# Attention loop of a two-layer block: value products one step later, two output units side by side, scores that wait tile by tile

## The reference

```
for i in range(1, N_BRANCH):
    acc = acc + jax.nn.sigmoid(proj(u, 'gate%d' % i)) * (ys[i] @ w_branch[i])
return acc @ w_out
```

## Time and profile before

| | |
|---|---|
| runs shown | 2553.7, 2552.97, 2550.1 us, median 2552.97 |
| the profiled execution | 2551.63 us, span 2549.8 us |
| mean granted TensorE clock | 0.988 |
| TensorE busy | 2430.2 us (95%) |
| VectorE busy | 1583.0 us (62%) |
| ScalarE busy | 1066.0 us (42%) |
| loop of A0 / B0 / C0 / D0 | 521 to 640 / 683 to 788 / 835 to 938 / 975 to 1052 us |
| loop of A1 / B1 / C1 / D1 | 1958 to 2043 / 2073 to 2131 / 2169 to 2224 / 2247 to 2294 us |

### The profile page before, as it was taken

The page is one execution under the profiler, slowest core; times in us unless marked ns, Lnnn a source line. Parts: engine busy times, 40 slices in busy tenths (PEclk is TensorE's granted clock), DMA queues, the critical chain, the costliest instruction groups (busy, mean ns, idle before and its releaser), DMA issues.

```text
span 2549.8 us, 31764 instructions
## 1 busy us (share of the span) xinstructions
PE 2430.2 (95%) x12584; PEld 1972.5 (77%) x12584; DVE 1583.0 (62%) x2620; ACT 1066.0 (42%) x1842; POOL 27.3 (1%) x43
## 2 busy tenths in 40 slices
PE   6999998999999999989999989999989999988998
PEld 3888886877767676668888868888868788768998
DVE  2799878345355447678898784333365466578654
ACT  5222234355444444462222342222354555556344
POOL 0000000000000000000000000000000000000000
PEclk9999999999999999999999999999999999998999
DMA  5555554221221112124555523222233243233554
GB/s 232 189 208 206 187 187 144 100 74 67 96 70 67 58 66 91 60 98 174 214 210 183 192 101 107 99 98 87 95 117 136 80 145 117 87 117 124 182 176 155
DMA packets 98069, 331.42 MB, mean 130 GB/s; under 512 B 11009, under 2 KB 12033, under 8 KB 97281
## 3 DMA queue, kind: packets, MB, share of 16 engines
q1 hardware_dynamic: 97922, 329.39, 36.7%
HBM read 323.06 MB, written 6.29 MB: 129 GB/s over the span
## 4 chain that ended last, share of the span: by engine, by line
PE 88%; DVE 5%; ACT 4%; issue 2%; DMA 1%; SPq 0%; POOL 0%; DVEq 0%; ACTq 0%
PE ps L347 26%; PE ps L338 24%; PE ps L339 23%; PE ps L649 5%; PE ps L1180 3%; PE ps L1155 3%; PE ps L1165 3%; ACT w_high L321 1%; ACT prob L1304 1%; DVE w_low L327 1%; DVE stat L1464 1%; DVE acc L1421 1%; DVE tmp L1418 0%; PE ps L548 0%; DMA mod_first<-in_mods 0%
## 5 line engine op out<-in xcount | busy, mean ns | idle before, releaser
L327 DVE TENSOR_TENSOR w_low<-raw,w_high 128x1024 fp32r<-128x1024 f32 (+1 forms) x488 | 551.2, 1135 | 519.7 <-ACT w_high L321 519.2
L321 ACT ACTIVATE w_high<-raw 128x1024 fp32r<-128x1024 f32 (+1 forms) x488 | 481.7, 990 | 764.8 <-DMA raw<-in_weights 764.6
L338 PE MATMUL ps<-u_high,w_high 128*128 128x512 f32 (+1 forms) x2208 | 771.4, 361 | 5.4 <-DVE hid_low L749 2.2
L339 PE MATMUL ps<-u_low,w_high 128*128 128x512 f32 (+1 forms) x2208 | 763.1, 357 | 0.0
L347 PE MATMUL ps<-u_high,w_low 128*128 128x512 f32 (+1 forms) x2496 | 541.6, 361 | 4.8 <-DVE w_low L327 4.8
L347 PEld LDWEIGHTS ps<-u_high,w_low 128*128 128x128 f32 x2496 | 421.4, 189 | 93.0 <-issue 18.6
L338 PEld LDWEIGHTS ps<-u_high,w_high 128*128 128x128 f32 x2208 | 418.9, 190 | 90.5 <-issue 19.2
L339 PEld LDWEIGHTS ps<-u_low,w_high 128*128 128x128 f32 x2208 | 419.2, 190 | 58.3
L410 DVE CUSTOM_DVE_ANT_0 ps<-mod_raw,c_all,smalls 128x1024 f32<-128x1024 f32 x256 | 319.3, 1288 | 1.4 <-DMA mod_raw<-in_mods 0.9
L338 PE MATMUL ps<-hid_high,w_high 128*128 128x512 f32 (+1 forms) x704 | 249.0, 363 | 0.0
L339 PE MATMUL ps<-hid_low,w_high 128*128 128x512 f32 (+1 forms) x704 | 249.0, 363 | 0.0
(11 more groups left out here) (147 smaller groups left out, 2258.8 us busy)
## 6 DMA issues: line engine op xcount, KB each, us to landing
raw<-in_weights SPq DMA_DIRECT2D x360, 512.0 KB, 3.5
mod_raw<-in_mods SPq DMA_DIRECT2D x128, 512.0 KB, 4.1
raw<-in_weights SPq DMA_DIRECT2D x64, 384.0 KB, 3.0
raw<-in_weights SPq DMA_DIRECT2D x64, 320.0 KB, 2.8
mod_first<-in_mods SPq DMA_DIRECT2D x16, 512.0 KB, 13.1
h_kept<-h SPq DMA_DIRECT2D x16, 256.0 KB, 2.0
na_bias<-in_na_rows SPq DMA_DIRECT2D x16, 256.0 KB, 4.1
h<-h_kept SPq DMA_DIRECT2D x2, 2048.0 KB, 9.8
```

The lines of the kernel that those rows point to most:

```text
L321: act.activation(w_high[s][:, 0:width], raw[s][:, 0:width], ACT.Copy).then_inc(high_made.sem, 1)
L327: dve.tensor_tensor(w_low[s][:, 0:width], raw[s][:, 0:width], w_high[s][:, 0:width], ALU.subtract).then_inc(low_made.sem, 1)
L338: pe.matmul(o, w_high[s][:, w], x_high(x), start=first and a == 0, stop=False)
L339: pe.matmul(o, w_high[s][:, w], x_low(x), start=False, stop=False)
```

## The change

Four edits. `scores(j)` waits for the keys and for the one query tile that it reads (`nk + t + 1` parts), and the single wait for all parts before the loop is gone. In B, C and D `mix(p)` runs in step 2p+3 and no longer in step 2p+2; A keeps its place. `high_of_out` and `low_of_out` move by the same step. In `Out` the high products of the first two units run interleaved, tile by tile, into banks 0 and 1, then the low products of both; the units from the third on are as before.

```
-                pe.wait_ge(self.part_made.sem, self.part_made.at(len(self.prep)))
                 pe.wait_ge(self.v_made.sem, self.v_made.at(4))
...
                 def scores(j):
                     t, q, key, nkeys = self.steps[j]
                     kt = t if self.nk == BT else 0
+                    pe.wait_ge(self.part_made.sem, self.part_made.at(self.nk + t + 1))
...
-                    if j % 2 == 0 and j:
-                        mix(j // 2 - 1)
+                    for p in self.mixes(j):
+                        mix(p)
                     flip(j)
...
+            def mixes(self, j):
+                after = 2 if self.b == "A" else 3
+                return [p for p in range(self.NP - 1) if 2 * p + after == j]
...
             def tensor(self, pe):
+                pe.wait_ge(high_made.sem, self.n0 + 2)
+                for k in range(KT):
+                    pe.wait_ge(self.merge.low.sem, self.merge.low.at(k + 1))
+                    for m in range(2):
+                        for x in (a_high, a_low):
+                            pe.matmul(ps[:, m, 0:self.T], w_high[SLOT_OF[self.n0 + m]][:, k], x[:, k, 0:self.T], start=k == 0 and x is a_high, stop=False)
                 for m in range(KT):
-                    if past(m - 1):
-                        pe.wait_ge(self.freed.sem, self.freed.at(m - 1))
...
+                    n, out = self.n0 + m, [(ps[:, m % 2, 0:self.T], [(k, k) for k in range(KT)])]
+                    if m < 2:
+                        product_low(pe, n, n, out, lambda k: a_high[:, k, 0:self.T])
+                        continue
+                    pe.wait_ge(self.freed.sem, self.freed.at(m - 1))
+                    product(pe, n, n, out, lambda k: a_high[:, k, 0:self.T], lambda k: a_low[:, k, 0:self.T])
```

More of the change, by code:

```diff
@@ L1352, in scalar @@
                     keep_probs(j)
-                    if j % 2 == 0 and j:
-                        high_of_out(j // 2 - 1)
+                    for p in self.mixes(j):
+                        high_of_out(p)
                     if b == "A":
@@ L1534, in vector @@
                             sub_low(p)
-                    elif j % 2 == 0 and j:
-                        low_of_out(j // 2 - 1)
+                    else:
+                        for p in self.mixes(j):
+                            low_of_out(p)
                     self.window_splits(dve, split_low, 2 + 2 * j)
@@ L1615, in tensor @@
             def tensor(self, pe):
-                for m in range(KT):
-                    if past(m - 1):
-                        pe.wait_ge(self.freed.sem, self.freed.at(m - 1))
[L1619 to L1622, removed]
+                pe.wait_ge(high_made.sem, self.n0 + 2)
[4 more added lines that the diff above has]
+                            pe.matmul(ps[:, m, 0:self.T], w_high[SLOT_OF[self.n0 + m]][:, k], x[:, k, 0:self.T], start=k == 0 and x is a_high, stop=False)
+                for m in range(KT):
+                    n, out = self.n0 + m, [(ps[:, m % 2, 0:self.T], [(k, k) for k in range(KT)])]
[4 more added lines that the diff above has]
+                    product(pe, n, n, out, lambda k: a_high[:, k, 0:self.T], lambda k: a_low[:, k, 0:self.T])
             def scalar(self, act):
```

## The result

| | before | after |
|---|---|---|
| median, us | 2551.68 (2550.1 to 2553.7, 4 runs) | 2536.33 (2535.57 to 2537.46, 4 runs) |
| profiled execution and its span | 2551.63, 2549.8 | 2537.46, 2535.7 |
| TensorE busy | 2430.2 (95%) | 2431.3 (96%) |
| mean granted clock | 0.988 | 0.987 |

The ratio of after to before is 0.9943 [0.9928, 0.9958]: faster by 0.57%, 15.3 us. The forecast was 2535, with 2528 to 2545 as its range. It was worked out against a before of 2552.97, the median of three runs; with a fourth run that median is 2551.68. So the forecast was 18.0 us less, and 15.3 (after) and 16.9 (e4) were measured.

The account below looks back on a forecast made before the run. TensorE, busy 95% of the span, was taken as the bound, so only its idle time could be gained. 2551.63 - 11.6 - 3.35 - 2.65 = 2534.0, with 1.34 for the median 2535.4, said as 2535; range 2531 to 2539, with rivals 2528 to 2545.

Parts of the forecast that it names:

- Scores' waits: Entrances of the eight branch loops: scores start earlier without waiting for all q copies, except D1 gains nothing; -11.6 us.
- No cost of waits that are met: Scores: 88 more waits were taken to cost nothing; upper bound 0.09 us each, 8 us in all.
- Late products: Value products one step later in B, C and D fill waits of short steps; -3.35 us in all.
- The clock's 0.4: D1's entrance: TensorE's idle time in one piece might halve the clock; +0.4 us, range nothing to 1.6.
- The tail's 0.85: Deep branches' tail: last product waits for the previous one's q_high and q_low after the last keep_probs; 0.85 us.
- window units would wait less for a bank: D1's loop: two window units no longer wait for a bank; -0.6 us.
- Out: First two output units side by side: 1.05 us gained in layer 0, 1.6 in layer 1; -2.65 us.
- (1): Rival: scores' gain real in only half the entrances, 11.6 becomes 6; time 2541, chance 0.18.
- (3): Rival: flips of even steps wait for probabilities, F2 in D1 a case; slower, up to 2584, chance 0.05.
- (2): Rival: full clock in B1 (1.5 us) and Out (1.3), D0's new waits don't come (1.4); 2531, chance 0.10.
- (4): Rival: no effect, entrances' time is given back before the loops end; 2550 to 2553, chance 0.05.
- The waits of scores for exponentials: Sign in TensorE's waits: those of scores for exponentials fall from 9.2 to about 5 us.

Follow-up runs that it names:

- e4: The changed kernel run once more, nothing edited; 2534.82 us, ratio 0.9938 to the kernel before.
- e1: Kernel before with only the scores' own waits for their tiles; 2542.17 us, ratio 0.9969.
- e7: Changed kernel with D1's first two row maxima on VectorE ahead of the two w_low; 2534.62 us, ratio 0.994.
- e8: Changed kernel with four more already met waits before each of the 96 scores; 2535.77 us, ratio 0.9941.
- e6: Changed kernel with high_of_out ahead of keep_probs in the deep branches; 2533.93 us, ratio 0.9934.
- e3: Kernel before with only Out's first two units side by side; 2548.39 us, ratio 0.9989.
- e9: Changed kernel with Out's first pair staggered: unit 0's tiles 0 to 5 don't wait for unit 1's high part; 2533.47 us, ratio 0.9932.
- e5: Changed kernel with value products late in B0 and C0 only, deep branches at the old step; 2532.12 us, ratio 0.9927.
- e2: Kernel before with only the value products and their two reads one step later; 2550.70 us, ratio 0.9999.
- e10: Changed kernel with the edits of e6, e7 and e9 together; 2533.55 us, ratio 0.9927.
- e12: Changed kernel with, unintentionally, all products at the old step, plus D0's q_high edit and those of e7 and e9; 2536.39 us, ratio 0.9948.

## Why the prediction was right

The time and the order of the terms came out: 2535 against 2536.33 and, again, 2534.82. Inside, two errors of 2.8 us and 0.8 us went against each other: by stages the terms made 15.9 for 17.6. That the time lies within 1.3 us of the forecast is in part luck, since before's own median fell by 1.3 and the half-clock stretches behind Out and at the norms move single executions by more than that. By its steps:

- **Scores' waits, forecast -11.6, measured -8.8** (stages of e1 without the norms; -9.5 by medians). The eight waits went, 11.8 in all, and seven of the eight were kept at the entrance, C0's half clock as well (its loop -1.38 for 1.6). D1's gain was given back, as said: S2 waits for a chain that starts with VectorE's two `w_low`, and e7 shows that this order is the cause. The error is a term that was not there: A1. Its S3 waits 2.08 us as before, but the granted clock behind it fell to 0.50 for 3.4 us in all 11 executions with the edit, and in none of the 3 without; A1's loop is 1.6 longer, more than the 1.15 that its entrance gained. D1 took 0.5 more than it got, and the loop of B0 is 0.32 longer in e1. I had priced the clock where an idle gap left or came, not where a gap stayed and only the time before it moved.
- **No cost of waits that are met.** Right, by e8.
- **Late products, forecast -3.35, measured -4.0** (e4 against e1). B0 -3.33 (forecast -2.85), C0 -1.81 (-1.40), D0 -0.44 (-0.7), B1 and C1 +0.15 each (0 and +0.4), D1 +1.28 (+0.8, and +0.4 for the clock). The clock's 0.4 did not come: e4 has half clock behind S2's wait and after has not, and their D1 loops are 49.44 and 49.41, because in e4 the waits of F0 (1.03) and F2 (0.48) are gone. The tail's 0.85 is right: M3 waits 1.94 for 1.11 before, and e6 takes it away, 0.78 in D0 and 1.10 in D1. F2 waits 0.48 for a forecast 0.5 (in after; in e4 it does not wait). Wrong in D1 was that window units would wait less for a bank: one waits 1.21 for 0.72 before, since ScalarE does exponentials and `keep_probs` ahead of its read.
- **Out, forecast -2.65, measured -2.8** (e3 and e4 by stages). In layer 0 -1.0 for -1.05, with the bank wait of 0.33. In layer 1 -1.8 for -1.6, but by another sum: I missed that the first unit now waits for the second's high part, 2.5 us; against that the pair behind it was 4.6 shorter, with half clock in 3.2 us for the 6.7 of the earlier trace rows. e9 takes the wait away and gains 1.08 on e4, but by the clock alone, as e5 and e6 show.
- **Rivals.** (1), half the scores' gain, is out: seven entrances kept theirs. (3), the flips of even steps, happened once, in D1's F2, with the price named. (2) came in one of its three parts, Out's half clock, which lasts 3.4 us for 6.9 from its beginning to its end; B1's stayed, and D0's new waits came. (4), no effect, is out by the intervals of the change and of e4.
- **Signs.** The waits of scores for exponentials fell from 9.2 to 7.1, not to about 5, by S2 in D1. F0 in D1 begins 8.86 us after the old place of S0, as forecast. No flip of B0 or C0 waits for probabilities.
- **What stands open.** Why A1's clock falls behind a wait that it outlived before. "TensorE: Matmul & The Clock Gate" of the Trainium skill, section "What's actually happening", has activity release the full rate; all 14 traces wait 2.1 us at the same place of the program, and differ in what lies before it (the nearest difference is the wait of S0 in A1, 1.08 us, some 18 us earlier, which the scores' edit took away), so the rule does not forbid this, but no run here tells what decides. No kernel was tried that changes the work before S3 alone.

## What to carry to other kernels

Give an instruction the wait for the one tile it reads, not for all of its group: a met wait costs nothing that can be measured, and seven of eight entrances gained their wait for the group (A1 lost it again to the clock). Moving work into a gap pays where the place it leaves has slack, so look at the slack of both places, stage by stage: late products gave 5 us in the two branches with few steps ahead, and cost time in three of the four with more. And look again at the order of the other engines after each such step: in D1 the edit of e7 alone gave 0.6 and that of e5 alone 1.3, both together 3.1.

## What the runs showed of the hardware that I had not expected

The granted clock behind a wait of TensorE is no function of that wait's length. Behind 2.07 to 2.09 us in A1 it fell in all 11 executions with the scores' edit, and behind the same 2.07 to 2.09 us in none of the 3 without (before, e2, e3). In C1 a wait of 2.5 us for `w_low` stands in all traces; from its last 0.6 us on, after, e6 and e10 ran 6.8 us at 0.50 and took 2.67 us longer, and e12 ran 3.4 us at 0.50 and took 1.19 longer, while e4, the same kernel as after, ran on. Stretch at the same place in e4, for the 2148.00 row above:

```profile
2144.30:2151.00 6.70, 4.18 (x35) 3.98 (x34) 6.13 (x13) 4.75 (x8) 0.88 (x1) 1.00 0.39 123
```

Two executions of one kernel so differ by 2.7 us at one place; the spread of the medians, some 1.5 us between the two sets of the changed kernel, is of this size.
